# Eight experts run as one uniform pipeline of weight units, with the first three units split earlier

## What is computed

```python
def swiglu(h, w1, w3, w2):
    return (jax.nn.silu(h @ w1) * (h @ w3)) @ w2

# layer 1: gates = softmax over the two best router logits of each token
for e in range(N_EXPERTS):
    y = swiglu(t, w1[e], w3[e], w2[e]).astype(f32)
    out = out + gates[:, e:e + 1] * y
```

## Time and profile before

| what | value |
|---|---|
| median of 3 runs | 1622.39 us (1618.79 to 1622.5) |
| the profiled execution's own time | 1622.69 us |
| its span, first to last instruction | 1620.8 us |
| PE busy over the span | 1521.1 us (94%) |
| DVE busy | 1258.9 us (78%) |
| ACT busy | 981.0 us (61%) |
| mean DMA rate over the span | 275 GB/s |
| the experts' matmuls, first to last start | 570.60 to 1591.31 us |

### The profile page before, as it was taken

The page is one execution under the profiler, slowest core; times in us unless marked ns, Lnnn a source line. Parts: engine busy times, 40 slices in busy tenths (PEclk is TensorE's granted clock), DMA queues, the critical chain, the costliest instruction groups (busy, mean ns, idle before and its releaser), DMA issues.

```text
span 1620.8 us, 23389 instructions
## 1 busy us (share of the span) xinstructions
PE 1521.1 (94%) x8402; PEld 1307.1 (81%) x8402; DVE 1258.9 (78%) x1228; ACT 981.0 (61%) x818; POOL 83.5 (5%) x63
## 2 busy tenths in 40 slices
PE   6999899998999789999999999999999999999992
PEld 4999899998999678878877877877877877877881
DVE  4887766666777488888878888888888878888885
ACT  4455433335354267777766776776767767767771
POOL 3000100000000110010010010010001001001000
PEclk9998999999998789999999999999999999999996
DMA  9541655454331389999989989999989999999972
GB/s 295 173 142 38 213 208 181 156 203 134 131 131 53 113 296 382 359 323 380 371 306 368 372 319 382 356 325 380 370 326 366 369 329 346 369 359 335 378 280 93
DMA packets 215253, 446.20 MB, mean 275 GB/s; under 512 B 7464, under 2 KB 63200, under 8 KB 214952
## 3 DMA queue, kind: packets, MB, share of 16 engines
q1 hardware_dynamic: 208176, 421.59, 72.1%
q0 software_dynamic: 5904, 21.74, 3.6%
q10 hardware_dynamic: 1136, 2.36, 0.4%
HBM read 433.98 MB, written 11.75 MB: 275 GB/s over the span
## 4 chain that ended last, share of the span: by engine, by line
PE 86%; DVE 7%; ACT 3%; issue 3%; DMA 1%; ACTq 0%; DVEq 0%; SPq 0%; POOLq 0%
PE ps L1321 26%; PE ps L1322 25%; PE ps L1323 25%; DVE w_lo L766 3%; ACT w_hi L494 2%; PE ps L1371 2%; PE ps L1640 2%; PE ps L1451 1%; PE ps L1337 1%; PE ps L1471 1%; PE ps L1565 1%; DVE x_tok L1302 0%; PE ps L1460 0%; DVE hF L787 0%; DVE rstd L784 0%
## 5 line engine op out<-in xcount | busy, mean ns | idle before, releaser
L766 DVE TENSOR_TENSOR w_lo<-raw,w_hi 128x2048 fp32r<-128x2048 f32 x401 | 911.9, 2290 | 199.7 <-ACT w_hi L494 191.8
L494 ACT ACTIVATE w_hi<-raw 128x2048 fp32r<-128x2048 f32 x401 | 763.5, 1918 | 247.5 <-PE ps L1323 246.0
L1321 PE MATMUL ps<-w_hi,xg 128*128 128x512 f32 x896 | 361.3, 403 | 10.1 <-DVE w_lo L766 10.1
L1323 PE MATMUL ps<-w_hi,xg 128*128 128x512 f32 x896 | 355.5, 397 | 0.0
L1322 PE MATMUL ps<-w_lo,xg 128*128 128x512 f32 x896 | 355.4, 397 | 0.0
L1321 PE MATMUL ps<-h_hi,w_hi 128*128 128x264 f32 x736 | 216.1, 294 | 17.4 <-DVE h_lo L793 15.1
L1321 PEld LDWEIGHTS ps<-w_hi,xg 128*128 128x128 f32 x896 | 169.1, 189 | 55.3 <-DVE w_lo L766 17.8
L1323 PE MATMUL ps<-h_hi,w_lo 128*128 128x264 f32 x736 | 211.7, 288 | 0.0
L1322 PE MATMUL ps<-h_lo,w_hi 128*128 128x264 f32 x736 | 211.6, 287 | 0.0
L1323 PEld LDWEIGHTS ps<-w_hi,xg 128*128 128x128 f32 x896 | 169.1, 189 | 40.9
L1322 PEld LDWEIGHTS ps<-w_lo,xg 128*128 128x128 f32 x896 | 169.3, 189 | 37.7
(11 more groups left out here) (268 smaller groups left out, 1436.0 us busy)
## 6 DMA issues: line engine op xcount, KB each, us to landing
raw<-in_moe_w_dram SPq DMA_DIRECT2D x336, 1024.0 KB, 6.0
raw<-in_ffn_w_dram SPq DMA_DIRECT2D x33, 1024.0 KB, 5.2
raw<-in_w_in_dram SPq DMA_DIRECT2D x24, 1024.0 KB, 5.4
raw<-in_w_out_dram SPq DMA_DIRECT2D x8, 1024.0 KB, 4.8
hstate<-in_state_hgrn_dram POOLq DMA_DIRECT2D x2, 2048.0 KB, 11.8
out_dram<-hstate POOLq DMA_DIRECT2D x2, 2048.0 KB, 9.2
y_pair<-y_rows POOLq DMA_DIRECT2D x2, 1024.0 KB, 6.2
x_rows<-in_x_prompt_dram SPq DMA_DIRECT2D x1, 1024.0 KB
```

Of the source, the lines that this page charges most:

```text
L494: act.activation(w_hi[:, s, :], raw[:, r, :], ACT.Copy).then_inc(hi_made, 1)
L766: dve.tensor_tensor(w_lo[:, s, :], raw[:, r, :], w_hi[:, s, :].bitcast(F32), ALU.subtract).then_inc(split, 1)
L1321: pe.matmul(out, l_hi, r_hi, start=start, stop=False)
L1323: return pe.matmul(out, l_lo, r_hi, start=False, stop=stop)
```

## The change

The next expert's first way up takes the place that a loop step's way up has: it stands between the last step's gate and that step's way down. So every step but the last of all has one form. Five things follow in the code.

- PE: `turn_slots` of the next expert moves one step forward, between the way up and the way down of the sixth step. The seventh step waits for `xg` and then multiplies the next expert's first way up.
- ACT: the silu of every step comes in the same place; `gather_high` stands ahead of the seventh step.
- DVE: `gather_low` stands ahead of the seventh step; the seventh gate stands behind the first `lo` of the next expert. `y_out` and `make_pick` move from the first way up into the first step, behind its gate, and this gate waits for the previous expert's way down (`FF_USED + 4` in place of `FF_USED + 2`).
- Start: units 0 and 1 of the first expert are split while the mixer's way out runs, unit 2 before the first gather; the block's number is read only after the first block, whose code stands apart from that of further blocks.
- SP's loads and POOL's stores and fetches keep their order.

```diff
@@ SP @@
+            def expert_block(b):
+                load_up(EX_BASE, 0, 0, b * BLOCK_STEPS)
+                with sp.Fori(0, EXPERTS - 1) as e:
+                    expert(b, e)
+                    i = b * BLOCK_STEPS + e * EX_STEPS + (EX_STEPS - 1)
+                    load_up(EX_BASE + 4, e + 1, 0, i)
+                    load_down(EX_BASE + 8, e, EX_STEPS - 1, i)
...
@@ ACT @@
-                if l == 0:
-                    hi(FF_BASE)
-                    hi(FF_BASE + 1)
+                hi(ob + OUT_UNITS)
+                hi(ob + OUT_UNITS + 1)
...
+            def expert(b, e):
+                i = b * BLOCK_STEPS + e * EX_STEPS
+                with act.Fori(1, EX_STEPS) as s:
+                    step(i + (s - 1))
+                gather_high(b * EXPERTS + e + 1)
...
+                    hi(EX_BASE + 2)
+                    gather_high(0)
...
@@ DVE @@
-                    if l == 0 and c in (3, 5):
-                        lo(FF_BASE + (c - 3) // 2)
+                    if c in (3, 5):
+                        lo(ob + OUT_UNITS + (c - 3) // 2)
...
-            slot_tokens(0)
+            slot_tokens(0, first=True)
+            lo(EX_BASE + 2)
...
+            def step(i, w3_used, it=None, e=None):
+                lo(EX_BASE + 4, i)
+                gate(i, w3_used)
+                if it is not None:
+                    y_out(it, i)
                     make_pick(it + 1, e + 1)
...
+                for j in range(1, 4):
+                    lo(EX_BASE + 4 + j, i)
+                turned_low(i)
+                lo(EX_BASE + 8, i)
+                if it is not None:
+                    slot_tokens(it + 1)
+                lo(EX_BASE + 9, i)
+
+            def expert(b, e, w3_used):
+                it, i = b * EXPERTS + e, b * BLOCK_STEPS + e * EX_STEPS
+                step(i, w3_used, it, e)
+                with dve.Fori(2, EX_STEPS) as s:
+                    step(i + (s - 1), (i + (s - 1)) * RAW + (FF_USED + 2))
+                gather_low(it + 1)
...
+                with dve.Fori(0, EXPERTS - 1) as e:
+                    n = i + e * EX_STEPS
+                    expert(b, e, n * RAW + (FF_USED + 4))
+                    n = n + (EX_STEPS - 1)
+                    step(n, n * RAW + (FF_USED + 2))
...
@@ PE @@
+            def step(i, it=None, e=None, turns=None, last=False):
+
+                pe.wait_ge(silu_done, i + 1)
+                up_half(b0, i, 0, 0)
+                up_half(b0 + 1, i, 0, 1)
+                turn(i)
+                up_half(b0 + 2, i, 1, 0)
+                up_half(b0 + 3, i, 1, 1)
+                if it is not None:
+                    find_slots(it + 1, e + 1)
+                    pe.wait_ge(y_ready, it * 2 + 2)
+                if turns is not None:
+                    turn_slots(turns)
+                down_half(b0 + 4, i, i, 0, it is not None, False)
+                down_half(b0 + 5, i, i, 1, False, last)
+
+            def expert(b, e):
+                it, i = b * EXPERTS + e, b * BLOCK_STEPS + e * EX_STEPS
+                step(i, it, e)
+                with pe.Fori(2, EX_STEPS - 1) as s:
+                    step(i + (s - 1))
+                step(i + (EX_STEPS - 2), turns=it + 1)
+                pe.wait_ge(xg_hi, it * 2 + 4)
+                pe.wait_ge(xg_lo, it * 2 + 4)
```

More of the change, by code:

```diff
@@ L353, in _ @@
                 with sp.Fori(1, nb) as b:
-                    with sp.Fori(0, EXPERTS) as e:
-                        expert(b, e)
+                    expert_block(b)
         @block.gpsimd
@@ new lines, in step, with expert_block @@
+            def step(i):
+                for j in range(4):
+                    unit(4 + j, i)
+                turned_high(i)
+                silu(i + 1, i * RAW + (FF_USED + 6))
+                unit(8, i)
+                unit(9, i)
+            def expert(b, e):
+                i = b * BLOCK_STEPS + e * EX_STEPS
+                with act.Fori(1, EX_STEPS) as s:
+                    step(i + (s - 1))
+                gather_high(b * EXPERTS + e + 1)
+            def expert_block(b):
+                i = b * BLOCK_STEPS
+                if isinstance(b, int):
+                    hi(EX_BASE + 2)
+                    gather_high(0)
+                for j in range(3 if isinstance(b, int) else 0, 4):
+                    unit(j, i)
+                silu(i, i * RAW + (FF_USED + 2))
+                with act.Fori(0, EXPERTS - 1) as e:
+                    expert(b, e)
+                    step(i + e * EX_STEPS + (EX_STEPS - 1))
+                expert(b, EXPERTS - 1)
+                unit(4, i + (BLOCK_STEPS - 1))
+                unit(5, i + (BLOCK_STEPS - 1))
+                turned_high(i + (BLOCK_STEPS - 1))
@@ L702, in _ @@
+            expert_block(0)
             act.wait_ge(blocks_ready, 1)
             nb = act.value_load(blocks_i[0:1, 0:1], min_val=1, max_val=3)
[L704 to L737, removed]
@@ L738, in _ @@
+            with act.If(nb > 1):
+                with act.Fori(1, nb) as b:
+                    expert_block(b)
             act.wait_ge(margin_ready, 1)
@@ L1240, in y_out @@
                                     ).then_inc(y_ready, 1)
[L1242 to L1250, removed]
-                    make_pick(it + 1, e + 1)
[L1252 to L1287, removed]
@@ L1616, in _, with up_half @@
             turn_slots(0)
+            def up_half(base, i, bank, half):
+                _, sl, _, _ = unit_of(base)
+                wh = w_hi[:, sl, :].rearrange("p (c n) -> p c n", c=4)
+                wl = w_lo[:, sl, :].rearrange("p (c n) -> p c n", c=4)
+                pe.wait_ge(split, i * RAW + (base + 1))
+                for c in range(4):
+                    k = 4 * half + c
+                    ins = mm3(ps[:, bank, :], xg[:, 0, k, :], xg[:, 1, k, :],
+                              wh[:, c, :], wl[:, c, :], k == 0, k == DC - 1)
+                ins.then_inc(used, 1)
@@ new lines, in turn, with down_half @@
+            def turn(s):
+                pe.wait_ge(g_done, START + s + 1)
+                pe.wait_ge(gT_split, START + s)
+                for j in range(4):
+                    ins = pe.transpose(ps[:, 2, P * j:P * j + P],
+                                       ex_g[:, P * j:P * j + P], ident[:, :])
+                ins.then_inc(g_turned, 1)
+            def down_half(base, i, s, half, first, last):
+                _, sl, _, _ = unit_of(base)
+                wh = w_hi[:, sl, :].rearrange("p (j n) -> p j n", j=2)
+                wl = w_lo[:, sl, :].rearrange("p (j n) -> p j n", j=2)
+                pe.wait_ge(split, i * RAW + (base + 1))
+                if half == 0:
+                    pe.wait_ge(gT_split, START + s + 1)
+                for j in range(2):
+                    k = 2 * half + j
+                    for n in range(2):
+                        ins = mm3(ps[:, 3 + n, :], gT[:, 0, k, :], gT[:, 1, k, :],
+                                  wh[:, j, 512 * n:512 * n + 512],
+                                  wl[:, j, 512 * n:512 * n + 512],
+                                  first and k == 0, last and k == 3)
+                ins.then_inc(used, 1)
@@ new lines, in expert, with expert_block @@
+            def expert(b, e):
[6 more added lines that the diff above has]
+                pe.wait_ge(xg_lo, it * 2 + 4)
+            def expert_block(b):
+                i = b * BLOCK_STEPS
+                if isinstance(b, int):
+                    pe.wait_ge(xg_hi, 2)
+                    pe.wait_ge(xg_lo, 2)
+                for j in range(4):
+                    up_half(EX_BASE + j, i, j // 2, j % 2)
+                with pe.Fori(0, EXPERTS - 1) as e:
+                    expert(b, e)
+                    step(i + e * EX_STEPS + (EX_STEPS - 1), last=True)
+                expert(b, EXPERTS - 1)
+                n = i + (BLOCK_STEPS - 1)
+                turn(n)
+                down_half(b0, n, n, 0, False, False)
+                down_half(b0 + 1, n, n, 1, False, True)
```

139 lines of the change are left out of this document (61 added, 78 removed).

## The result

The changed kernel took 1636.87 us (median of 4 runs, 1636.41 to 1641.63) beside 1622.45 us for the kernel before (4 runs, 1618.79 to 1622.84). The ratio is 1.0101 with a 95% interval of 1.0077 to 1.0124: slower by 1%, clear of the 0.3% that a measurement of this kernel can tell. Forecast were 1610 us, 1602 to 1619 in the range, and 0.05 for slower. The profiled execution took 1636.69 us, with a span of 1634.9.

A forecast was written before the change was run, and what follows sets the result against it. PE was taken to bound the experts. From 1622.7 us, seven expert passages gain 10.2, vanished clock dips 3.4, and the start loses 0.3: 1609.4, forecast as 1610, range 1602 to 1619.

The forecast's parts named there:

- the end of an expert: Last step of each expert: waits for the gate and the turned result's split, 3.15 us, go; last expert's end unchanged.
- the first step's hold: Second unit of an expert's first step: PE stands 2.1 us for the split, plus 0.1 for a slow matmul.
- The store: slot_tokens needs the previous y_rows store landed: forecast at 14.6 us from PE's first unit, 12.5 behind y_out's end; nothing taken.
- A tie: Store landing at 14.6 us against PE's slot search at 13.7 to 14.9: nothing taken, 0.7 us as upper bound.
- the store decides: Rival: a later store landing holds back split and PE eight times; slower from 13.8 us, 1629 at 14; chance 0.05.
- The clock: Half-clock stretches behind expert ends: the two dips go, gaining 2 x 1.7 = 3.4 us, and none are expected.
- The rival on the clock: The new 2.1 us hold brings half clock: 1623 with 8 x 1.7 us, 1614.5 with three dips; chance 0.12.
- The start: First expert, three units split early: first matmul at 568.8 instead of 570.60 us, then a 2.1 hold; net 0.3 lost.
- What was spare: Gather to gather forecast at 125.4 us; the gather before the next expert's first split fits with 0.2 us to spare.
- Code fetched anew: Rival: PE's longer expert loop no longer fits, six jumps back stop PE up to 3.3 us each, 1629; chance 0.05.

The follow-up runs named there:

- run 1: Changed kernel with slot_tokens moved from an expert's first step to its second, behind the last split: 1610.19 us, 0.9937 of the kernel before.
- Run 3: Changed kernel plus one DVE semaphore wait between the second and third split of an expert's first step, same order: 1613.01 us, 0.9958 of the kernel before.
- run 2: Changed kernel with the gate in an expert's first step moved behind the second split, parting the w_lo: 1600.6 us, 0.9884 of the kernel before.
- run 4: Changed kernel with the first three units split behind the gather again, as in the kernel before: 1635.82 us, 1.0093 of the kernel before.

## Why the prediction was wrong

Two mechanisms that I saw were there: **the end of an expert** (both waits gone) and **the first step's hold** (2.12 and 0.1 more, as worked out). The steps that failed:

- **The store.** "A tie: I take nothing, and 0.7 as the upper bound." The landing 11.6 us behind the issue was carried over as if it were a property of the transfer. It holds POOL's 4.97, and these depend on how many splits stand behind `y_out` in one run: the change made it three. That is 2.2 more on POOL and, with 0.5 more of flight, 14.3 to the landing. The search did come where it was forecast: in the expert shown it ends at 982.0 us, and the store lands at 970.36 + 14.34 = 984.7. As `slot_tokens` has the last split of the step behind it, PE paid for it: of the 37.0 us that it waited for splits behind 600 us, seven first holds (six of 2.12, one of 1.96) are 14.7, and the other 22.3 are eight second holds. Less 0.28 each that were there before, these are 20.1 us. My rival "the store decides" had the place and the price (slower from 13.8 us on), and got 0.05, because I held nine stores under full load against it. They were under full load of the DMA engines; beside three `w_lo` was none of them. Nor are the 3.3 and 11.6 us that I read as an idle and a busy DMA all load: 0.98 and 4.97 of them are POOL's instruction.
- **The clock.** "... without these I expect none" had no case for holds that were new. In runs 1 and 3 six of eight first holds (2.12 us, the last 1.96 or 1.97) are followed by half the clock, in run 2 (1.46) none. With one more at the last end, eight stretches at 1.57 are 12.6 us, where I had none. The rival on the clock had its price nearly right, at 8 x 1.7, and took it for the only thing that could go wrong. These two terms make 20.1 + 12.6 = 32.7 us, 5.4 more than the 27.3 between 1609.4 and 1636.7 that are to be explained.
- **The start.** The first matmul was forecast for 568.8 and came at 567.32, but the early split that I costed has no part in it that run 4 could tell; 2.0 us stood there already in the first mixer. The half clock also lasts 6.8 us there in place of 10.2. So at the second unit of the first way down PE is 2.7 us ahead of the kernel before, if the second hold is left out (601.26 - 2.85 = 598.41, against 601.09), where I had it 0.3 behind: 3.0 us.
- **What was spare.** Run 3 has the change's order and no late store. Two of its gathers, with no half clock between them, are 1186.64 - 1061.51 = 125.13 us apart, where I had 125.4: 7 x 0.27 = 1.9 us. With the 3.0 of the start this is 4.9 of the 5.4 by which the two terms overshoot.
- **Code fetched anew** did not show: no wait of PE between 600 and 1590 us stands at a loop's end.

That run 1 hits the forecast of 1610 is chance. Its seven stretches at half clock (six behind first holds, one at the last end) cost 11.0 us that the forecast did not have. Against them stand the 3.0 of the start and 7 x 0.85 = 6.0 of shorter experts (124.55 us in place of 125.4), part of which is the edit's own, as it also takes away the 0.28 us at the second unit of the way down.

The Trainium skill (SBUF — State Buffer, section Who interferes with whom) says that a VectorE instruction with two SBUF inputs and a GpSimd instruction that reads SBUF exclude each other, and the later one waits in full. Here `w_lo` has two SBUF inputs, the gate one, and POOL ends 0.85 to 0.89 us behind a `w_lo` whether the gate, a gap or the split of `gT` follows, so the trace agrees that these two block each other. The same section also says that `tensor_tensor`, which `w_lo` is, did not stall a DMA in a probe; here it does (7.16 us beside three, 0.98 beside none), and the measurement decides. The rule speaks of one instruction; in this trace the store was kept waiting over three.

## What to carry to other kernels

The time from the issue to the landing of a DMA that POOL issues is not one number: split it into the issuing engine's instruction and the flight, and ask what stands beside the instruction in the new order. Where an engine runs the same operation several times without a gap, try a semaphore wait of 0.1 us or another operation in between: here either let the blocked engine through. And where a forecast ends in a tie, price both outcomes for the whole loop, and move the later reader off it: here the slot numbers had time, for the rows that POOL began to fetch by them at 986.26 us were turned by PE only at 1072.86.

## What was not expected of the hardware

- POOL does not get in between `w_lo` instructions that follow without a gap when it works on the store (7.16 us beside three), and it does with a gap of 0.12 us (2.76).
- For the fetch of `xg_tok` it does get in (rows below): its instruction takes 2.34 us and ends 0.83 behind the first of two `w_lo`. In the order of the code a loop begins between those two, but the trace shows no gap (4.49 us for both, as elsewhere). Why store and fetch differ stays open.
- The flight behind the end of POOL's instruction is no constant either: in the first seven experts 7.1 to 7.4 us in the changed kernel, 5.6 to 5.9 in runs 2 and 3.
- Which of two holds brings half the clock is not told by its length alone. In the changed kernel all first holds but one are followed by full clock, and the second hold, 15 us later, by half in six of eight experts. Why was not tried.

For the second point, here are DVE, then POOL, of the changed kernel in the expert shown above:

```profile
985.48 4.49 DVE L792 TENSOR_TENSOR w_lo<-raw,w_hi 128x2048 fp32r<-128x2048 f32 x2
```
```profile
986.26 2.34 POOL L446 DMA_INDIRECT xg_tok<-h_rows,slot_tok  x1 [8.74 <-DVE slot_tok L1217]
```
